# Slot 0's operands ahead of the routing weights in a mixture-of-experts layer

## The reference, cut to what matters

```python
g_logits = un @ w_group + b_group;  p_group = softmax(g_logits);  g_sel = argmax(g_logits)
e_sel = (un @ w_route + b_route) of group g_sel;  top_v, top_i = top_k(e_sel, 2)
top_w = softmax(top_v) * p_group[g_sel]        # two routing weights for each token
h = silu(un @ w_gate[e]) * (un @ w_up[e])      # 256 wide, for the two chosen experts e
y = sum over the two of top_w * (h @ w_down[e])
x = layer_norm(ALPHA * x + (1 + gate) * y)
```

## Time and profile before

| | us |
|---|---|
| three timed runs | 1362.06, 1362.23, 1363.22 (median 1362.23) |
| the profiled execution, its own time | 1362.96 |
| its span, first to last instruction | 1361.2 |
| TensorE busy | 1240.9 (91%) |
| DVE busy | 928.6 (68%) |
| ScalarE busy | 503.2 (37%) |
| GpSimd busy | 355.0 (26%) |

### The profile page before, as it was taken

How to read it: one execution, slowest core, us unless ns; L and a number is a source line. 1 busy time by engine, 2 the same in 40 slices (tenths; PEclk the granted TensorE clock), 3 DMA queues, 4 the chain that set the end, 5 groups by cost and what they waited for, 6 DMA issues and landing times.

```text
span 1361.2 us, 23166 instructions
## 1 busy us (share of the span) xinstructions
PE 1240.9 (91%) x6695; PEld 977.1 (72%) x6696; DVE 928.6 (68%) x1827; ACT 503.2 (37%) x936; POOL 355.0 (26%) x439
## 2 busy tenths in 40 slices
PE   6796899999999997999999729999999999999596
PEld 1122599999999986888877528888888888888342
DVE  1105559888988898989899985565665556523188
ACT  1010444355444643211111024454654454422175
POOL 0004021122202243221211023343445445432100
PEclk9897899999999998999999859999999999999798
DMA  8992010222202435544343368777998888864673
GB/s 264 392 343 74 1 40 18 75 92 92 61 31 92 170 105 182 171 146 164 124 140 126 116 215 264 216 200 207 273 296 214 248 257 254 255 166 88 182 297 147
DMA packets 119241, 231.36 MB, mean 170 GB/s; under 512 B 11413, under 2 KB 70041, under 8 KB 119157
## 3 DMA queue, kind: packets, MB, share of 16 engines
q1 hardware_dynamic: 105375, 180.50, 38.6%
q0 software_dynamic: 13824, 50.34, 16.1%
HBM read 161.49 MB, written 69.97 MB: 170 GB/s over the span
## 4 chain that ended last, share of the span: by engine, by line
PE 66%; DVE 19%; issue 5%; ACT 4%; DMA 3%; SPq 1%; POOL 1%; DVEq 0%; ACTq 0%; POOLq 0%
PE bank L1536 17%; PE bank L1538 17%; PE bank L1537 17%; PE bank L1483 5%; PE bank L1510 5%; PE bank L1603 2%; DVE ada_arena L1464 1%; DVE arena L1183 1%; DMA arena<-in_w_in 1%; DVE arena L1057 1%; PE bank L1557 1%; DVE arena L1071 1%; PE bank L1674 1%; DVE ada_arena L1450 1%; DMA ada_arena<-in_w_ada 1%
## 5 line engine op out<-in xcount | busy, mean ns | idle before, releaser
L1536 PE MATMUL bank<-parts 128*128 128x256 f32 (+2 forms) x1472 | 512.1, 348 | 19.2 <-DVE parts L1380 9.8
L1538 PE MATMUL bank<-parts 128*128 128x256 f32 (+2 forms) x1472 | 496.8, 337 | 0.0
L1537 PE MATMUL bank<-parts 128*128 128x256 f32 (+2 forms) x1472 | 496.2, 337 | 0.0
L1536 PEld LDWEIGHTS bank<-parts 128*128 128x128 f32 x1472 | 282.5, 192 | 51.5 <-issue 13.9
L1538 PEld LDWEIGHTS bank<-parts 128*128 128x128 f32 x1472 | 282.2, 192 | 28.8
L1537 PEld LDWEIGHTS bank<-parts 128*128 128x128 f32 x1472 | 282.8, 192 | 25.9
L1483 PE MATMUL bank<-ident,arena 128*128 128x128 f32 (+4 forms) x788 | 116.9, 281 | 13.6 <-DMA arena<-u_d,tok_i 6.0
L1483 PEld LDWEIGHTS bank<-ident,arena 128*128 128x128 f32 (+4 forms) x788 | 94.1, 146 | 40.2 <-DVE parts L1048 7.7
L1373 DVE TENSOR_TENSOR parts<-arena,parts x90 | 104.9, 1221 | 14.8 <-ACT parts L885 14.3
L1385 DVE TENSOR_TENSOR arena<-arena,bank 128x256 f32<-128x256 f32 x48 | 20.2, 421 | 133.2 <-ACT arena L895 130.7
L1510 PE MATMUL bank<-ada_arena,cT 128*9 128x512 f32 x192 | 85.8, 609 | 15.8 <-DMA ada_arena<-in_w_ada 15.8
(11 more groups left out here) (254 smaller groups left out, 1856.9 us busy)
## 6 DMA issues: line engine op xcount, KB each, us to landing
ada_arena<-in_w_ada SPq DMA_DIRECT2D x12, 2048.0 KB, 11.7
arena<-in_w_gate SPq DMA_DIRECT2D x16, 1024.0 KB, 5.9
arena<-in_w_up SPq DMA_DIRECT2D x16, 1024.0 KB, 12.7
arena<-in_w_down SPq DMA_DIRECT2D x16, 1024.0 KB, 14.6
y_d<-zero SPq DMA_DIRECT2D x17, 512.0 KB, 6.2
arena<-in_x_prompt SPq DMA_DIRECT2D x8, 1024.0 KB, 7.0
yT_d<-arena SPq DMA_DIRECT2D x16, 512.0 KB, 4.6
arena<-yT_d SPq DMA_DIRECT2D x16, 512.0 KB, 6.1
```

The source lines that it names most:

```text
L1536: pe.matmul(out, x_hi, w_hi, start=start, stop=False)
L1537: pe.matmul(out, x_hi, w_lo, start=False, stop=False)
L1538: return pe.matmul(out, x_lo, w_hi, start=False, stop=stop)
```

## The change: what it does

On DVE, all one-hot rows `hot_a` leave `rows_of` and the place behind `slots_ready`. The new order there is: expert 0's four gate/up low parts, three register loads, the low parts of slot 0's tokens, all 34 rows `hot_a`, the first half of the routing weights, `hidden(0)`, the tokens of slot 1, expert 0's two down low parts, `hT_evac(0)`, the second half of the weights, and only then the low parts of expert 1. The sums of `slot_weights` go behind slot 3's tokens, and `y_evac(0)` and `y_evac(1)` stand behind them. ScalarE makes slot 0's tokens before the two Exps. GpSimd gathers slots 2 and 3 before its three products for the slot weights. TensorE multiplies the slot weights after `turn_x(3)`, ahead of `down(1)`, and no longer after `turn_x(1)`. `hot_a` and `hot_s` lie elsewhere in memory, where tiles of the norm stage were; hence the new waits on the stores `x1_st` and `u2_st`.

```diff
-        hot_a, hot_t, hot_p = (ada_at(20480 + n * 2176, 2 * NT * P // 2).bitcast(BF16).rearrange("p (k t r) -> p k t r", k=2, t=NT)
-                               for n in range(3))
+        hot_t, hot_p = (ada_at(20480 + n * 2176, 2 * NT * P // 2).bitcast(BF16).rearrange("p (k t r) -> p k t r", k=2, t=NT)
+                        for n in (1, 2))
+        hot_a = at(16896, 2 * NT * P // 2).bitcast(BF16).rearrange("p (k t r) -> p k t r", k=2, t=NT)
-        hot_s = ada_at(19456, NT * SLOTS).bitcast(BF16).rearrange("p (k t s) -> p k t s", k=2, t=NT)
+        hot_s = at(14984, NT * SLOTS).bitcast(BF16).rearrange("p (k t s) -> p k t s", k=2, t=NT)
...
@@ GpSimd @@
+            for s in (2, 3):
+                pool.wait_ge(S["xgT_mm"], 2 * s - 2)
+                gather(s, s % 2)
             pool.wait_ge(S["wpart_ready"], 1)
...
             pool.tensor_tensor(hot_s, hot_s, by_tok(w_part[2]), ALU.mult).then_inc(S["hotw_ready"], 1)
-            for s in (2, 3):
-                pool.wait_ge(S["xgT_mm"], 2 * s - 2)
-                gather(s, s % 2)
...
@@ ScalarE @@
             slots = [next_expert(s) for s in range(3)]
             x_evac(0)
+            act.wait_ge(S["w_exp"], 1)
+            act.activation(g_dif, g_dif, ACT.Exp).then_inc(S["w_expd"], 1)
+            act.wait_ge(S["w_exp"], 2)
+            act.activation(d_12, d_12, ACT.Exp).then_inc(S["w_expd"], 1)
             silu(0, 0)
             x_evac(1)
             hT_evac(0)
             split_next(slots[0], range(GU_PARTS))
+            silu(1, 1)
+            x_evac(2)
+            split_next(slots[0], range(GU_PARTS, E_PARTS))
+            hT_evac(1)
+            split_next(slots[1], range(GU_PARTS))
+            silu(2, 0)
+            x_evac(3)
+            split_next(slots[1], range(GU_PARTS, E_PARTS))
             act.wait_ge(S["wslot_ok"], 1)
-            for s in (1, 2):
...
+            y_evac(0, 0)
+            y_evac(1, 1)
+            hT_evac(2)
+            split_next(slots[2], range(GU_PARTS))
...
@@ DVE, rows_of @@
-                if n < 3:
-                    plain_rows(n)
...
@@ DVE, ahead of hot_s @@
+            dve.wait_ge(S["x1_st1"], 16 * (NT // 2))
...
@@ DVE, behind slots_ready @@
-            plain_rows(3)
-            plain_rows(4)
+            dve.wait_ge(S["slots_ready"], 1)
+            split_first(range(GU_PARTS))
+            slots = [next_expert(s) for s in range(3)]
+            x_evac(0)
+            for b, n in ((0, NT // 2 + 1), (1, NT // 2)):
+                dve.wait_ge(S[f"u2_st{b}"], 16 * n)
+            for n in range(len(BATCHES)):
+                plain_rows(n)
...
-            split_first(range(GU_PARTS))
+            hidden(0, 0)
+            x_evac(1)
+            split_first(range(GU_PARTS, E_PARTS))
+            hT_evac(0)
...
+            split_next(slots[0], range(GU_PARTS))
+            hidden(1, 1)
+            x_evac(2)
+            split_next(slots[0], range(GU_PARTS, E_PARTS))
+            hT_evac(1)
+            split_next(slots[1], range(GU_PARTS))
+            hidden(2, 0)
+            x_evac(3)
+            split_next(slots[1], range(GU_PARTS, E_PARTS))
             slot_weights()
...
+            y_evac(0, 0)
+            y_evac(1, 1)
+            hT_evac(2)
+            split_next(slots[2], range(GU_PARTS))
...
@@ TensorE @@
             turn_x(1, 1, 1)
-            slot_weights(2)
-            slot_weights(1).then_inc(S["wslot_mm"], 1)
             turn_h(0)
             for s in (1, 2):
                 gate_up(s, s % 2)
                 turn_x(s + 1, (s + 1) % 2, (s + 1) // 2 + 1)
+                if s == 2:
+                    slot_weights(2)
+                    slot_weights(1).then_inc(S["wslot_mm"], 1)
                 down(s - 1, first=s == 1)
                 turn_h(s)
```

More of the change, by code:

```diff
@@ L867, in _ @@
                 act.activation(w_hi[:, 0, cols], w_raw[0][:, cols], ACT.Copy).then_inc(S["w_hi"], 1)
[L869 to L872, removed]
             def next_expert(s):
@@ L913, in _ @@
             split_next(slots[0], range(GU_PARTS))
-            act.wait_ge(S["wslot_ok"], 1)
-            for s in (1, 2):
[L916 to L921, removed]
+            silu(1, 1)
[6 more added lines that the diff above has]
+            split_next(slots[1], range(GU_PARTS, E_PARTS))
+            act.wait_ge(S["wslot_ok"], 1)
+            y_evac(0, 0)
+            y_evac(1, 1)
+            hT_evac(2)
+            split_next(slots[2], range(GU_PARTS))
             with act.Fori(1, SLOTS // 2 - 1) as j:
@@ L1408, in _ @@
             dve.wait_ge(S["slots_ready"], 1)
+            split_first(range(GU_PARTS))
             slots = [next_expert(s) for s in range(3)]
             x_evac(0)
-            split_first(range(GU_PARTS, E_PARTS))
+            for b, n in ((0, NT // 2 + 1), (1, NT // 2)):
+                dve.wait_ge(S[f"u2_st{b}"], 16 * n)
+            for n in range(len(BATCHES)):
+                plain_rows(n)
+            gl, el = logits[:, :, 0:NGR], logits[:, :, NGR:NR]
+            o.step(dve.tensor_reduce(g_max, gl, axis=AX, op=ALU.max))
@@ L1412, in _ @@
+            g_dif3 = g_dif.rearrange("p (t g) -> p t g", g=NGR)
+            dve.tensor_tensor(g_dif3, gl, bc(g_max, NGR), ALU.subtract).then_inc(S["w_exp"], 1)
+            o.step(dve.tensor_tensor(prod_w, e_all, el.unsqueeze(1).to_broadcast([P, 2, NT, NE]), ALU.mult))
+            o.step(dve.tensor_reduce(m_12.rearrange("p (k t) -> p k t", k=2), prod_w, axis=AX, op=ALU.add))
+            dve.tensor_tensor(d_12, m_12[:, NT:2 * NT], m_12[:, 0:NT], ALU.subtract).then_inc(S["w_exp"], 1)
             hidden(0, 0)
@@ L1413, in _ @@
             x_evac(1)
-            slot_weights()
[L1415 to L1423, removed]
+            split_first(range(GU_PARTS, E_PARTS))
+            hT_evac(0)
+            dve.wait_ge(S["w_expd"], 2)
@@ new lines, in _ @@
+            o.did(dve.tensor_reduce(w_sum, g_dif3, axis=AX, op=ALU.add))
+            o.step(dve.tensor_scalar(m_12[:, 0:NT], d_12, 1.0, None, ALU.add))
+            o.step(dve.tensor_tensor(w_sum, w_sum, m_12[:, 0:NT], ALU.mult))
+            o.step(dve.reciprocal(wgt[:, 0, :], w_sum))
+            o.step(dve.tensor_tensor(wgt[:, 1, :], wgt[:, 0, :], d_12, ALU.mult))
+            o.step(dve.tensor_copy(w_part[0], wgt[:]))
+            o.step(dve.tensor_tensor(w_rest, wgt[:], w_part[0], ALU.subtract))
@@ new lines, in _ @@
+            o.step(dve.tensor_copy(w_part[1], w_rest))
+            o.step(dve.tensor_tensor(w_rest, w_rest, w_part[1], ALU.subtract))
+            dve.tensor_copy(w_part[2], w_rest).then_inc(S["wpart_ready"], 1)
+            split_next(slots[0], range(GU_PARTS))
[7 more added lines that the diff above has]
+            split_next(slots[1], range(GU_PARTS, E_PARTS))
```

## The result

| | before | after |
|---|---|---|
| median of the timed runs, us | 1363.22 (1362.06 to 1364.56) | 1369.51 (1368.56 to 1370.53) |
| ratio to before, with its 95% interval | | 1.0046 [1.0032, 1.0061] |
| the profiled execution, its own time | 1362.96 | 1369.13 |
| its span | 1361.2 | 1367.4 |

The change makes the kernel slower by 0.46%, 6.3 us. The traces differ by 6.2, and the mark (the start of gate_up(3)) went from 843.69 to 849.33, by 5.6. Behind the mark the two traces lie within 0.6 us of each other, so nearly all of it is ahead.

What follows compares the result with a forecast made beforehand. TensorE was taken to bound the 48 slots, with DVE the chain ahead of them. The steps moved gate_up(3) from 843.7 to 853.6, +9.9 us; from 1362.96 that makes 1372.9, less 0.7 for timed runs: 1372, range 1365.5 to 1375.5.

Steps and rivals of the forecast that it cites:

- Step 1: Norm stage: eight one-hot rows ahead of the last tile's norm come off the path, mark -1.4 us; earlier batches' rows give 0.
- Step 2: Ahead of slot 0: rows and weights, 5.6 us, go behind the tokens on DVE; gate_up(0) starts at 806.1.
- Step 3: Slot 0: silu 0.9 us late behind Exp and table load; gate_up(1) starts at 817.9, 7.1 ahead.
- Step 4: Slot 1: expert 1's four low parts and three GpSimd products take turns, 13.1 us against 4.6; TensorE stands 10 us.
- Step 5: Slot 2: low clock loses 2.5 us, slot weights 2.4, wait at down(1) 1.7; gate_up(3) starts at 853.6.
- A: Slot 1: no turn-taking on the path, DVE's four parts run in 4.6 us; -1.1 us, 1361; chance 0.10.
- B: Slot 1: DVE's four parts keep GpSimd out until they are done; +1.4 us, 1363.6; chance 0.08.
- Rival C: Scatters: all of the forecast, and the scatters become late too, adding 3 us; 1375; chance 0.06.
- Rival D: Ahead of gate_up(2): TensorE's idle is there but the clock isn't lost; +7.4 us, 1369.6; chance 0.16.

Runs made afterwards that it cites:

- e6: Kernel before with only the 26 one-hot rows taken out of `rows_of` and put behind `slots_ready`; ratio 0.9997 to before, 1363.44 us.
- e5: Kernel before's order up to slot 0's tokens, but all 34 rows behind `slots_ready` and the late place of the slot weights' sums; ratio 1.0034 to before, 1367.85 us.
- e7: Changed kernel with the first half of the weights ahead of the 34 rows on DVE; ratio 1.0033 to before, 1368.53 us.
- e1: Changed kernel with GpSimd's three one-hot products covering one tile of 17, a memset added, result incomplete; ratio 0.9966 to before, 1359.37 us.
- e2: Changed kernel with `hidden(1)` and slot 2's tokens ahead of expert 1's four gate/up low parts on DVE; ratio 0.9979 to before, 1361.12 us.
- e10: e9 with all 34 one-hot rows moved behind slot 2's tokens, none between or behind the weight halves; ratio 0.9937 to before, 1355.58 us.
- e9: e8 with GpSimd's three products ahead of its gather of slot 3; ratio 0.9989 to before, 1362.49 us.
- e3: Changed kernel with 36 unused matmuls between down(0) and turn_h(1) to fill TensorE's idle time; ratio 1.0029 to before, 1367.80 us.
- e8: Changed kernel with both weight halves during slot 0, 16 rows behind slot 2's tokens, slot weights ahead of `turn_x(3)`; ratio 0.9979 to before, 1361.64 us.

## Why the prediction was right, and where its sizes were off

It forecast 1372.0, +9.9 at the mark; +6.2 came in the profiled execution, +5.6 at the mark. The mechanism was the one forecast, and direction and range held. At the mark the sum was 4.3 too high: 3.9 from the head (steps 1 and 2), 0.6 from step 3 and 0.7 from step 4, less 0.9 that step 5 had too low. By its steps, each as the time by which the place is moved:

| place | predicted | measured |
|---|---|---|
| gate_up(0) | -7.0 | -10.9 |
| gate_up(1) | -7.1 | -11.6 |
| gate_up(2) | +3.3 | -1.8 |
| gate_up(3) | +9.9 | +5.6 |

**Step 1, the term that was mis-sized.** -1.4 stood for the rows, -3.5 came. The eight rows ahead of the last norm paid as said: its first DVE instruction is at 763.72 for 767.57, 1.4 of it from these rows. But the 18 rows of the earlier batches weren't free (e6: 3.7 for 26 rows of 4.3). What DVE gained there it passed on: its instruction L1210 (L1215 after) of the tenth tile is at 674.40 for 676.51 before, that of the last tile 3.9 earlier.

**Step 2.** The other 2.0 of the head: the three register loads had cost 2.0 idle us and were charged again; the tokens' low parts follow the gate/up parts at 800.52 with no idle time at all. In e5, which has the old order, the 2.01 are back. That the loads run under the four parts is a guess; the runs show only the place. The work moved behind (5.6) was right at 5.4.

**Step 3.** silu(0) was late behind the table load by 1.6, not 0.9 (it starts at 810.89, and would have 0.43 behind the start of gate_up(0)'s last product, at 809.29). gate_up(0) took 7.1 us to that point and not 8.2: only seven of its products ran at the low clock, where twelve had. TensorE had stood 2.0 us ahead of it, not 9.0. gate_up(0) to (1) came out at 11.3 for the 11.8 forecast. e7 shows the place.

**Step 4, where the gain is lost: right.** Its sum gives 10.5 us of standing (837.7 - 827.2), which it rounds to 10. GpSimd started at 817.81 with the parts at 818.15; they took 12.5 for the 13.1 forecast, TensorE stood 9.1, and from gate_up(1) to (2) it is 19.1 for 19.8. e1 shows that it is the length of the products, e2 that it is the order of DVE's queue behind the parts, and e10 that bank readers aren't touched. Rivals A and B are out: in A the parts would keep 4.6, in B GpSimd would have waited. The border set for the forecast, gate_up(2) at 832 or later, was met by half a microsecond, since the head had moved 4 us further than counted: that this sign held is luck.

What the Trainium skill (SBUF — State Buffer, "A bandwidth-pool intuition that's wrong") says of an exclusive lock agrees with this trace: at half speed for both, the parts would have been done about 3 us sooner (an estimate: twice 4.63 from 818.15 is 827.4, and they ended at 830.7), and in e9 a row of 0.17 us would not have taken 2.9.

**Step 5.** The clock at gate_up(2) cost 1.4, not 2.5 (e3). The slot weights took 2.5 and the wait at down(1) 1.9, for 2.4 and 1.7. Not forecast was the low clock inside down(1), another 1.5, for which the runs show no rule (below). From gate_up(2) to (3) it is 16.8 us for 9.3 before, 7.5 more where 6.6 were forecast.

Rival C (late scatters) didn't come: the second starts at 852.75 and no evacuation waits. Rival D (clock kept) hits the time, 1369.6 for 1369.51, but by luck: the clock was lost, and the head was better. In e3, which kept it at gate_up(2), the stretch behind is 1.4 shorter.

## What to carry to other kernels

An edit that brings an engine forward brings its collisions forward: look up what each engine issues at the new time, and whether an instruction that others wait for stands behind the one that will be held. Work on SBUF alone on DVE should not be queued ahead of urgent work while GpSimd has long instructions; work that reads a bank may be. Here the order that pays gives GpSimd its long products when DVE stands idle or has mostly bank readers to do (e10), and it took the order of both queues to get there (e8, e9).

## What the runs showed of the hardware that was not expected

- The turns between DVE and GpSimd are by instruction, not by time. Parts of 1.2 us beside products of 2.9 took 3.7 to 3.9, and three one-hot rows of 0.17 us took 2.9 to 3.0, each next to one product (e9). For its own length the short one loses most. In e8 the first down part sat through two products, 7.15 us; why it missed its turn is open.
- The clock fell inside down(1) in the kernel after and in e3, behind 68 small products and 1.86 us of waiting; in e1, e5 and e7 it stayed full with the same products and 1.86 or 1.87 of waiting, and in e10 with 1.17. TensorE had stood 8.3 us ahead of gate_up(2) in the kernel after and in e7, not in e3, e1 or e5, so that doesn't sort them. What makes the difference is open; the 1.5 us that it cost the kernel after may not come in every execution.
- Three register loads on DVE cost 2.0 us ahead of the tokens in one order (before, e5, e6) and nothing in the other, where four parts of 4.6 us stand just ahead.
